# A hybrid decoder step on one core: state space norm taken group by group behind the loop, output products begun between the value units, three units issued by GpSimd

## What is computed

```python
xn = rmsnorm(x, g_mix); proj = xn @ w_in          # q, k, v, z, x/B/C, dt
attn = rmsnorm(attend(q, k, v), g_attn)           # samples attend to 256 cached rows
y, ssm = ssd_scan(conv(x), dt, a, B, C, state)
y = (y + d_skip * x) * silu(z)
y = rms(y in 2 groups of 512) * g_ssd             # a mean of squares for each group
h = x + concatenate([attn, y]) @ w_out
h = h + peer_ffn(rmsnorm(h, g_ffn)); out = rmsnorm(h, g_final)
```

## Time and profile before

| | us |
|---|---|
| median of 3 runs (lowest, highest) | 1196.28 (1191.41, 1199.67) |
| the profiled execution's own time | 1196.83 |
| its span, first to last instruction | 1194.8 |
| TensorE busy, share of the span | 1150.9 (96%) |
| VectorE, ScalarE, GpSimd busy | 788.4, 568.3, 744.7 |

### The profile page before, as it was taken

One profiled execution on the slowest core, in us unless ns is written; L12 is line 12 of the kernel. 1 busy time (PEld: TensorE's weight loads), 2 busy tenths in 40 slices (PEclk: granted clock), 3 DMA queues, 4 the chain that ended last, 5 costly groups with the idle time before them and its releaser, 6 DMA issues.

```text
span 1194.8 us, 24222 instructions
## 1 busy us (share of the span) xinstructions
PE 1150.9 (96%) x7585; PEld 1012.7 (85%) x7585; DVE 788.4 (66%) x1722; ACT 568.3 (48%) x1282; POOL 744.7 (62%) x621
## 2 busy tenths in 40 slices
PE   8999999839999999999999999999999999999997
PEld 7877777509979999999999999998888888888876
DVE  6689786783179999100899999994445546666534
ACT  3323223442345555565555554444555555555545
POOL 0066350024726799889666666666767788789654
PEclk9999999857999999999999999999999999999999
DMA  7568666772644476666544554444665688778643
GB/s 251 169 214 274 204 204 202 262 260 67 188 142 142 136 201 185 186 177 194 150 141 143 143 141 143 143 140 142 193 188 189 187 303 273 237 275 290 194 157 107
DMA packets 109179, 225.13 MB, mean 188 GB/s; under 512 B 12754, under 2 KB 21570, under 8 KB 108586
## 3 DMA queue, kind: packets, MB, share of 16 engines
q1 hardware_dynamic: 105858, 212.60, 57.3%
q0 software_dynamic: 2304, 8.39, 2.0%
q10 hardware_dynamic: 936, 3.14, 0.7%
HBM read 215.80 MB, written 8.19 MB: 187 GB/s over the span
## 4 chain that ended last, share of the span: by engine, by line
PE 70%; issue 1%; DVE 0%; POOL 0%; ACT 0%; DVEq 0%; POOLq 0%; ACTq 0%
PE bank L1616 30%; PE bank L1646 30%; PE bank L1626 5%; PE bank L1569 2%; PE bank L1581 1%; PE bank L1593 1%; PE bank L1666 0%; PE bank L1683 0%; POOL hl L1509 0%; DVE acts L2042 0%; PE bank L1674 0%; ACT acts L1852 0%; POOL hl L1494 0%; PE bank L1701 0%; PE bank L1659 0%
## 5 line engine op out<-in xcount | busy, mean ns | idle before, releaser
L1494 POOL TENSOR_TENSOR hl<-ring,hl 128x512 fp32r<-128x512 f32 x448 | 586.0, 1318 | 184.6 <-ACT hl L1732 176.1
L1732 ACT CAST hl<-ring 128x512 fp32r<-128x512 f32 x512 | 317.1, 620 | 290.4 <-PE bank L1646 156.3
L1616 PE MATMUL bank<-split,hl 128*128 128x256 f32 x3072 | 378.4, 282 | 0.4 <-ACT hl L1732 0.3
L1616 PEld LDWEIGHTS bank<-split,hl 128*128 128x128 f32 x3072 | 366.2, 188 | 0.9 <-issue 0.5
L1646 PE MATMUL bank<-hl,split 128*128 128x512 f32 x1524 | 353.6, 394 | 0.0
L1646 PEld LDWEIGHTS bank<-hl,split 128*128 128x128 f32 x1524 | 286.0, 188 | 67.7 <-issue 0.9
L501 PE MATMUL pj<-xn,ring 128*128 128x264 f32 x672 | 158.4, 392 | 0.7 <-ACT proj L778 0.7
L2012 DVE TENSOR_TENSOR split<-acts,split 128x256 fp32r<-128x256 f32 x128 | 129.4, 1036 | 39.5 <-ACT split L1828 35.1
L501 PEld LDWEIGHTS pj<-xn,ring 128*128 128x128 f32 x672 | 126.2, 192 | 24.9 <-issue 4.6
L2019 DVE TENSOR_TENSOR hl<-ring,hl 128x512 fp32r<-128x512 f32 x64 | 45.2, 706 | 117.6 <-ACT hl L1732 117.6
L483 POOL TENSOR_TENSOR wo<-ring,wo 128x512 fp32r<-128x512 f32 x32 | 42.2, 1325 | 106.5 <-ACT wo L930 106.4
(11 more groups left out here) (355 smaller groups left out, 1096.3 us busy)
## 6 DMA issues: line engine op xcount, KB each, us to landing
ring<-in_uv SPq DMA_DIRECT2D x256, 256.0 KB, 2.8
ring<-in_v_rows SPq DMA_DIRECT2D x256, 256.0 KB, 3.3
ring<-in_w_ring SPq DMA_DIRECT2D x76, 512.0 KB, 4.0
room<-in_cache_k SPq DMA_DIRECT2D x64, 128.0 KB, 3.8
room<-in_cache_v SPq DMA_DIRECT2D x28, 256.0 KB, 3.3
hs<-in_state_ssm SPq DMA_DIRECT2D x8, 512.0 KB, 5.0
out_ssm_s<-hs SPq DMA_DIRECT2D x8, 512.0 KB, 6.0
acts<-x_rows SPq DMA_DIRECT2D x8, 512.0 KB
```

Source lines behind the costliest of these rows:

```text
L1494: nc.gpsimd.tensor_tensor(hl[:, r % HL, 1], raw[:, r], hl[:, r % HL, 0].bitcast(F32), ALU.subtract).then_inc(lo_done, 1)
L1616: mm = nc.tensor.matmul(out, hl[:, r % HL, m, k * P:(k + 1) * P], split[:, x, kk, 0:TP], start=(kk == 0 and n == 0), stop=(kk == KD - 1 an ...
L1732: nc.scalar.copy(hl[:, r % HL, 0], raw[:, r]).then_inc(hi_done, 1)
```

## The change

The state space norm is taken in two groups. Silu of both groups comes right behind the last copy of the loop (`gates`), ahead of the samples' exponents; the gate products come ahead of `masked(7)`; squares and slab sums of group 0 come ahead of `normal(7)`, its sum over partitions ahead of `turn_probs(7)`, and group 1 follows behind `value_unit(2)`. The first six state space halves of the output products are begun behind `value_unit(4)`, and units 5, 6 and 7 and the prompt attention's norm lie between them. Units 3, 4 and 6 are issued by GpSimd, unit 6 between its second and third low part; unit 2 and unit 6 have a new home in `xn`. `late_sums` comes one half later, and the banks are renamed to fit.

```diff
-        sq_ssd = xn
...
-        V_HOME = (2, 3, 0, 1, 2, 0, 1, 2)
+        val_homes.append(part(xn[:].rearrange("p k n -> p (k n)"), 0, SIDE, D // 2))
+        V_HOME = (2, 3, 4, 0, 1, 2, 4, 0)
+        sq0 = part(flatp, 0, 3, NT)
+        sq1 = part(ssd, 24 * P - 4 * NT, 4, NT)
...
-        out_bank = [pj[0], pj[1], yb, swb, xbp, bcp, hd[1], hd[0]]
+        out_bank = [pj[0], pj[1], bcp, xbp, swb, yb, hd[1], hd[0]]
...
 SP
-                values(3)
                 sp.wait_ge(ys_done, KD)
                 for j in range(SIDE):
                     sp.dma_start(sel6[j * SPAN:j * SPAN + NH], t["sel"]).then_inc(sel6_in, 16)
-                for n in range(4, VU):
-                    values(n)
+                values(5)
+                values(7)
...
 GpSimd
+                def values(n):
+                    q, m, g = n // (2 * NPG), n // NPG % 2, n % NPG
+                    pool.wait_ge(unit_used, {3: KU - 1, 4: KU, 6: KU + 3}[n])
+                    for j in range(SIDE):
+                        b = q * SIDE + j
+                        at = pool.value_load(ptab[0:1, b * NPG + g:b * NPG + g + 1], min_val=0, max_val=t["n_pool"] - 1)
+                        pool.dma_start(val_homes[V_HOME[n]][:, j],
+                                       t["cache_v"][bass.ds(at, 1)].rearrange("a p n -> p (a n)")[:, m * 4 * P:(m + 1) * 4 * P]
+                                       ).then_inc(val_full[n], 16)
+                pool.wait_ge(ptab_in, 16)
+                values(3)
+                values(4)
                 for n in range(2 * N_OUT):
+                    if n == 2:
+                        values(6)
                     pool.wait_ge(o_hi, n + 1)
...
 TensorE
                 turn_sample_probs()
+                pe.wait_ge(pre_s, 1)
+                pe.wait_ge(own_copied, 1)
+                nc.tensor.matmul(pj[1][:, 0:NT], ones, sq0[:, 0], start=True, stop=True).then_inc(sum_s, 1)
                 turn_probs(KD - 1)
                 pe.wait_ge(h1_done, KD)
                 value_unit(0)
                 value_unit(1)
                 attend(KD - 1)
                 value_unit(2)
+                pe.wait_ge(pre_s, 2)
+                nc.tensor.matmul(pj[0][:, 0:NT], ones, sq1[:, 0], start=True, stop=True).then_inc(sum_s, 1)
                 value_unit(3)
                 pe.wait_ge(y_done, KD)
                 value_unit(4)
-                pe.wait_ge(own_copied, 1)
-                pe.wait_ge(pre_s, 1)
-                for n in range(GROUPS):
-                    mm = nc.tensor.matmul(pj[n][:, 0:NT], ones, sq_ssd[:, 4 * n], start=True, stop=True)
-                mm.then_inc(sum_s, 1)
-                value_unit(5)
-                pe.wait_ge(o_copied, 2 * KD)
-                pe.wait_ge(pre_p, 1)
-                nc.tensor.matmul(hd[0][:, 0:TP], ones, sq_att[:, 0, 0:TP], start=True, stop=True).then_inc(sum_p, 1)
-                value_unit(6)
-                value_unit(7)
...
+                        if half:
+                            pe.wait_ge(mix_lo, a + 1)
...
                 pe.wait_ge(pj_copied, N_IN)
+                pe.wait_ge(sums_read, 2)
+                out_half(N_IN, 0, 1, True, False)
+                value_unit(5)
+                pe.wait_ge(o_copied, 2 * KD)
+                pe.wait_ge(pre_p, 1)
+                nc.tensor.matmul(hd[0][:, 0:TP], ones, sq_att[:, 0, 0:TP], start=True, stop=True).then_inc(sum_p, 1)
+                out_half(N_IN + 1, 1, 1, True, False)
+                value_unit(6)
                 values(0)
-                for d in range(6):
-                    pe.wait_ge(mix_lo, 2)
-                    if d == 4:
-                        late_sums()
-                    out_half(N_IN + d, d, 1, True, False)
-                    if d == 0:
-                        values(1)
-                        spread_rates()
+                out_half(N_IN + 2, 2, 1, True, False)
+                value_unit(7)
+                out_half(N_IN + 3, 3, 1, True, False)
+                values(1)
+                spread_rates()
+                out_half(N_IN + 4, 4, 1, True, False)
+                late_sums()
+                out_half(N_IN + 5, 5, 1, True, False)
...
 ScalarE (gates and squares are new)
+                def gates(n):
+                    act.wait_ge(pj_copied, CONV_CH + 16 * n + 16)
+                    k = slice(Z0 + 4 * n, Z0 + 4 * n + 4)
+                    nc.scalar.activation(proj[:, k], proj[:, k], ACT.Silu).then_inc(z_done, 1)
+                def squares(n):
+                    act.wait_ge(gated, n + 1)
+                    if n == 0:
+                        act.wait_ge(st_done, KD)
+                        nc.scalar.activation(sq0, mix[:, KD:KD + 3], ACT.Square)
+                        nc.scalar.activation(mix[:, KD - 1], mix[:, KD + 3], ACT.Square).then_inc(sq_s, 1)
+                    else:
+                        act.wait_ge(pre_s, 1)
+                        nc.scalar.activation(sq1, mix[:, KD + 4:MIXC], ACT.Square).then_inc(sq_s, 1)
...
 VectorE (gate is new: one product of mix and proj for a group)
+                    if c == KD - 1:
+                        gate(0)
+                        gate(1)
                     masked(c)
...
+                sample_rates()
+                dve.wait_ge(sq_s, 1)
+                link(nc.vector.tensor_tensor(sq0[:, 0], sq0[:, 0], sq0[:, 1], ALU.add),
+                     nc.vector.tensor_tensor(sq0[:, 2], sq0[:, 2], mix[:, KD - 1], ALU.add))
+                nc.vector.tensor_tensor(sq0[:, 0], sq0[:, 0], sq0[:, 2], ALU.add).then_inc(pre_s, 1)
+                normal(KD - 1)
...
+                ssd_factor(0)
+                dve.wait_ge(sq_s, 2)
+                link(nc.vector.tensor_tensor(sq1[:, 0:2], sq1[:, 0:2], sq1[:, 2:4], ALU.add))
+                nc.vector.tensor_tensor(sq1[:, 0], sq1[:, 0], sq1[:, 1], ALU.add).then_inc(pre_s, 1)
+                ssd_factor(1)
+                ssd_scaled(0)
+                ssd_scaled(1)
```

More of the change, by code:

```diff
@@ L901, in sample_exps @@
                                          accum_out=s6[:, 2, b:b + 1]).then_inc(exp6, 1)
+                gates(0)
+                gates(1)
                 for b in range(NQ):
@@ L1258, in _, with ssd_factor @@
-                dve.wait_ge(root_p, 1)
-                for k in range(KD):
-                    nc.vector.scalar_tensor_tensor(out=mix[:, k, 0:TP], in0=mix[:, k, 0:TP], scalar=par[:, P_GAT + k:P_GAT + k + 1],
-                                                   in1=rr[:, 0, 0:TP], op0=ALU.mult, op1=ALU.mult).then_inc(mixed_p, 1)
+                def ssd_factor(n):
+                    dve.wait_ge(sum_s, n + 1)
+                    nc.vector.tensor_scalar(tmp[:, n], pj[1 - n][:, 0:NT], GROUPS / D, EPS, ALU.mult, ALU.add).then_inc(sums_read, 1)
+                    dve.wait_ge(sums_read, n + 1)
+                    nc.vector.reciprocal(tmp[:, n], tmp[:, n]).then_inc(var_s, 1)
@@ new lines, in ssd_scaled @@
+                def ssd_scaled(n):
+                    dve.wait_ge(root_s, n + 1)
+                    for k in range(4 * n, 4 * n + 4):
+                        nc.vector.scalar_tensor_tensor(out=mix[:, KD + k], in0=mix[:, KD + k], scalar=par[:, P_GSSD + k:P_GSSD + k + 1],
+                                                       in1=tmp[:, n], op0=ALU.mult, op1=ALU.mult).then_inc(mixed_s, 1)
+                dve.wait_ge(qk_ready, 2 * KD)
+                ssd_factor(0)
+                dve.wait_ge(sq_s, 2)
```

96 lines of the change are left out of this document (45 added, 51 removed).

## The result

| | before | after |
|---|---|---|
| median (lowest to highest; 4 runs each, one chip), us | 1197.97 (1191.41 to 1200.73) | 1185.06 (1184.66 to 1185.51) |
| profiled execution, its span, us | 1196.83, 1194.8 | 1185.12, 1182.9 |
| the stretch (below), us | 102.14 | 91.16 |

The ratio of the times is 0.9892, 95% interval 0.9861 to 0.9924: 1.1% faster, 12.9 us by the medians. 1187 was forecast. The interval stands clear of 1, so the gain can be told from nothing, which the prediction had doubted.

The account below looks back on a forecast made before the run. TensorE waits some 45 us, VectorE bounding the last half, at a low clock. First output product at 251.9 and later terms put the end at 319.6 against 329.3: gain 9.7, less 0.7, from 1196.28 gives 1187, range 1181 to 1193.

Parts of the forecast that it names:

- d0: First state space output half on TensorE: to begin at 251.9 instead of 273.93 and run at the low clock to 257.2.
- d1: Second state space output half, behind unit 5 and the attention's sum: to end at 263.4, including a wait of 1.6.
- d4: Fifth state space output half: 2.0 idle ahead, for ScalarE's high part 8, then low clock behind thin products, to 286.1.
- Steps 1 to 4: From 227.24: gates, exponents and squares, slab sums, then TensorE's work through the sum of group 1, ending at 243.9.
- step 4: TensorE from 236.0 to 243.9: sum of group 0, turned probabilities, units 0 and 1, `attend`, unit 2, sum of group 1.
- Step 5: VectorE ahead of the first output half: mean 0.4, reciprocal 1.8, scalings 3.2, `mix_low` 1.2, to 250.5; low part added, 251.9.
- the lock's cost: VectorE and GpSimd take turns at a shared port pair ahead of the first output half: one low part, 1.3.
- The wait in d1: Second output half waits 1.6 for low part 2, behind unit 6's four transfers on GpSimd at 1.7 each.
- a wait for POOL's low part in d1: Named sign in the second output half: TensorE would wait 1 to 2 us for GpSimd's low part.
- The clock helps and nothing waits: Rival: GpSimd transfers cost 1.0, no wait in d1, clock back earlier in d0 and d4; gain 13.5, 1183; chance 0.17.
- Halves at the low clock: Rival: d1 and the third, fourth and sixth output halves also take 5.3; 9.5 lost, gain 0, 1196; chance 0.10.
- Transfers hold up the low parts: Rival, two forms: GpSimd transfers at 3 us, gain 4, 1192, chance 0.10; at 3.6, gain zero, costlier slower, chance 0.07.

Follow-up runs that it names:

- e1: Changed kernel with all eight value units issued by SP again, in order, none by GpSimd: 1186.99 us, ratio 0.9912 to the kernel before.
- e4: Changed kernel with ScalarE's high parts of weights 0 and 1 moved behind those of `mix`, so GpSimd's low parts start later: 1186.58 us, ratio 0.9931.
- e5: Changed kernel with the sum of the attention's squares moved behind the second output half on TensorE: 1184.46 us, ratio 0.9912.
- e6: Changed kernel with ScalarE's high parts of weights 8 and 9 moved ahead of its wait for the samples' attention: 1181.90 us, ratio 0.9898.
- e2: Changed kernel with value units 5 to 7 and the attention's sum put back ahead of the first output half: 1192.41 us, ratio 0.9964.
- e3: Changed kernel with the sum of group 1 moved ahead of `attend` and value unit 2 on TensorE: 1184.55 us, ratio 0.9893.
- e7: Changed kernel with Silu behind the exponents, both groups' gates behind `normal(7)`, sum of group 0 behind value unit 1: 1189.39 us, ratio 0.9932.
- e10: Changed kernel with the edits of e1, e5 and e6 together: 1182.59 us, ratio 0.9881.
- e12: e11 plus five products of constants, which nothing reads, behind value unit 4: 1179.34 us, ratio 0.9869.
- e11: e10 plus weights 0's high part cast between the two high parts of `mix`, the other weights behind: 1178.67 us, ratio 0.986.
- e8: Changed kernel with seven products of 384 columns of constants, which nothing reads, behind value unit 4: 1186.88 us, ratio 0.9934.

## Why the prediction was right, step by step

It held: 1187 was forecast with 1181 to 1193, 1185.06 came. The most likely size, a change within 1%, was just missed by the ratio (0.9892, interval 0.9861 to 0.9924). By the stretch 9.0 to 9.7 were forecast and 10.98 came. Dates of the forecast less 227.14, and of the profile after less 226.10:

| | forecast | measured |
|---|---|---|
| d0 begins | +24.8 | +26.2 |
| d1 ends | +36.3 | +37.9 |
| d3 ends | +46.9 | +47.9 |
| spread ends | +51.7 | +51.4 |
| d4 begins | +53.7 | +53.4 |
| d5 ends | +63.2 | +62.0 |
| last product ends | +92.5 | +91.2 |

- **Steps 1 to 4.** Right: `masked` at 228.53 (229.6, less the shift of 1.0), turned probabilities 5.2 us later than before ("some 5.5 us later"; +9.5 against +4.3), sum of group 1 done at +17.3 (243.9: +16.8), the clock rising within unit 1. The terms named in step 4 add up to 8.6, though, and not to the 7.9 between 236.0 and 243.9; without the 0.69 of the wait the pieces took 8.1. Not foreseen: these 0.69 for unit 2's transfers, which come late beside GpSimd's (e1).
- **Step 5.** The eight scalings took 5.25, not 3.2, and the lock's cost, which I put at one low part (1.3), was 2.02 for two (e4). d0 is 1.4 late for this and for unit 2.
- **The wait in d1.** 1.6 was forecast, 2.02 came, but for another reason: not low part 2 behind unit 6's transfers on GpSimd (0.96 to 1.15 for each, not 1.7), but the attention's slab sums on VectorE: 5.9 us beside four low parts, 3.3 (2.91 and 0.43) in e4 beside fewer. Alone, in the kernel before, they took 2.4. I had taken the sum's input as there. e5 shows it: the sum moved, and the wait went. The two errors nearly cancel, so that this term came out is luck. One of the signs that were named, a wait for POOL's low part in d1, did not show.
- **d4.** Right: 2.0 forecast, 1.93 measured, released by ScalarE's cast, and the low clock for the reason given, the thin products ahead (5.3; 5.20). The edit of e6 takes the wait away; the low clock stays in three of four kernels with it.
- **Where the 1.3 us too little came from.** `spread_rates` 2.05, not 2.94, and d5 with the late sums 3.7, not 4.2; no other half fell to the low clock, for which I had taken off 0.7.
- **What the sum did not name.** It priced TensorE's pieces one by one, the units at 0.9 to 1.0 in place of 1.91, and so had the clock in it. But it said nowhere that 6.6 of the 11 us are the same products at a higher clock, and that only 4.4 are idle time.
- **Rivals.** *The clock helps and nothing waits*: its price for GpSimd's issue was nearly right (1.15 against its 1.0), but VectorE took the wait's place. *Halves at the low clock*: d1, d2, d3 and d5 ran in 3.14 to 3.52. *Transfers hold up the low parts*, in both forms: a transfer would have had to cost 3 us; four took 3.85 (249.71 to 253.56). e1 shows the change in who issues to be worth nothing or slightly less.

Open: why executions of e2, e3, e4, e6, e7, e10 and e12 spread over 6 to 10 us when the changed kernel's lie within 1 to 3, why the clock stayed up in e6, and how much of unit 2's wait (0.26 to 3.71 in the profiles where GpSimd issues) each of the queues beside it causes. The gain of 10.98 is split by e2: 5.6 to 6.2 for the order of the halves, all of it idle time. In e2's kernel the rest against the kernel before is 4.8: 6.5 less for the same products at a higher clock, and 1.7 more of idle time. This rest, the norm by groups ahead of the value units and the early Silu, was not tried alone.

## What to carry to other kernels

When a wait for a chain on a full engine is filled with the next stage's work, look at what the chain is made of: only the part that the next stage needs should stand in front. Then look at the small operations that were hidden before: one cast in the wrong place cost 1.93 of idle time. Read busy time as well as idle time: here more was gained by the clock than by the waits. And where VectorE is the bound, give GpSimd its work just behind the operations that are waited for (e11: eight scalings in 3.22), not beside them (5.25).

## What the runs showed of the hardware

- A direct transfer of 256 KB issued by GpSimd at an address from a register keeps it for 0.54 us, with 1.15 from one to the next. It lands after 5.9 to 10.6 us, where SP's into `room` take 3.1 at the median in the same kernel, most of them at other times. SP's four for unit 2, issued at the same time as GpSimd's, take 7.8 at the median, and 5.3 where GpSimd issues none (e1).
- Each low part of GpSimd that lies beside VectorE's scalings costs VectorE 1.0 us (5.25 against 3.23 for eight); a product of two columns beside six low parts in a row took 6.57, until the last had ended (e4).
- The granted clock is still 1.0 in a whole us without work at 252, and 0.50 at 254, 2.35 us idle behind dense work at the full clock (e8). The half behind it takes 4.67, where with no idle time it takes 3.58 (e12).
- Thin products of 4 and 16 columns are followed by a half at the low clock, with an idle time of 1.93 between (5.20, changed kernel) and with none: 5.31 before, 4.67 to 4.78 in e10 to e12. In one profile of fourteen it stayed at the full clock (3.15, e6). The 16 products of 4 columns alone (1.95, `values(0)`) are followed by a half of 3.14.
